# A two-block transformer on one core: attention heads of the second block beside its projections, and stage seams taken token tile by token tile

## The reference, cut to what matters

```python
# mixer A, token width 1024: 4 "diff" heads with two softmax maps each, 4 "moba" heads
h = x @ w_in                                  # 1024 x 3072
dq, dk, mq, mk = (apply_rope(...) of slices of h);  dv, mv = slices of h
s = where(kpos <= qpos, q @ k.T * scale, -inf);  p = softmax(s)
w = p[:, :, 0] - lam_full * p[:, :, 1]        # diff: the two maps joined
a = rms_norm_2(w @ dv, subln) * (1 - lambda_init)
b = softmax(causal(mq @ mk.T * scale)) @ mv   # moba: with 256 tokens one block, plain causal attention
x = layer_norm(ALPHA * x + concat(a, b) @ w_out)
x = layer_norm(ALPHA * x + square(relu(x @ w1)) @ w2)          # FFN, inner width 4096
# mixer B, gated linear attention (GLA): q, k (512 wide), v, r (1024), 16 gate columns
g = log_sigmoid(h16 @ w_gate_up + b_gate) / 16                  # decay of every key column
o = causal linear attention of q, k, v with the decays exp(cumsum(g))
x = layer_norm(ALPHA * x + (rms_norm_2(o) * silu(r)) @ w_out)
x = layer_norm(ALPHA * x + square(relu(x @ w1)) @ w2)           # second FFN; its result is the output
```

## Time and profile before

| | |
|---|---|
| median of three runs | 1716.16 us (1713.0 to 1716.29) |
| the profiled execution | 1713.44 us, of which the span from first to last instruction is 1711.6 us |
| mean granted clock of TensorE in it | 0.940 of full speed |
| PE busy | 1380.6 us (81% of the span) |
| DVE busy | 1131.3 us (66%) |
| ACT busy | 539.2 us (32%) |
| POOL busy | 454.7 us (27%) |
| weights and experts read from HBM | 431.00 MB, 252 GB/s over the span |

### The profile page before, as it was taken

One profiled execution on the slowest core, in us unless ns is written; L12 is line 12 of the kernel. 1 busy time (PEld: TensorE's weight loads), 2 busy tenths in 40 slices (PEclk: granted clock), 3 DMA queues, 4 the chain that ended last, 5 costly groups with the idle time before them and its releaser, 6 DMA issues.

```text
span 1711.6 us, 17345 instructions
## 1 busy us (share of the span) xinstructions
PE 1380.6 (81%) x6264; PEld 971.9 (57%) x6264; DVE 1131.3 (66%) x2051; ACT 539.2 (32%) x1023; POOL 454.7 (27%) x393
## 2 busy tenths in 40 slices
PE   6976788777777677777777788658999899789998
PEld 5875668523223232222222267547999687679996
DVE  6655665688887788886555556647756659577564
ACT  2453434222221213212111233323434246234341
POOL 1154305244443443544444200000211025001110
PEclk9988899999998999999999989878999999889999
DMA  9554526799999999999999823204555534245550
GB/s 367 190 184 148 196 74 227 293 421 409 421 421 412 421 408 382 400 422 420 422 421 421 344 75 123 98 25 142 182 196 197 189 110 147 75 151 179 188 197 25
DMA packets 116629, 433.17 MB, mean 253 GB/s; under 512 B 6832, under 2 KB 7088, under 8 KB 83520
## 3 DMA queue, kind: packets, MB, share of 16 engines
q0 software_dynamic: 36864, 268.45, 38.0%
q1 hardware_dynamic: 79392, 162.51, 26.8%
q10 hardware_dynamic: 288, 1.11, 0.2%
HBM read 431.00 MB, written 1.05 MB: 252 GB/s over the span
## 4 chain that ended last, share of the span: by engine, by line
PE 47%; DMA 23%; DVE 19%; ACT 6%; issue 2%; POOL 2%; SPq 0%; DVEq 0%; ACTq 0%; POOLq 0%
PE PS L45 45%; DMA EB<-in_experts,EI 22%; DVE EB L78 5%; DVE WL L75 3%; ACT BIG L24 2%; PE PS L84 1%; DVE X L63 1%; POOL W L75 1%; ACT WH L24 1%; DVE Y L75 1%; DMA W<-in_w_ada 1%; DVE GV L75 1%; DVE EB L63 1%; DVE XL L75 1%; DVE ST L69 1%
## 5 line engine op out<-in xcount | busy, mean ns | idle before, releaser
L45 PE MATMUL PS<-EB,BIG 128*128 128x512 f32 x1024 | 495.4, 628 | 169.9 <-ACT BIG L24 169.8
L45 PEld LDWEIGHTS PS<-EB,BIG 128*128 128x128 f32 x1024 | 190.3, 197 | 470.3 <-ACT BIG L24 287.3
L78 DVE CUSTOM_DVE_ANT_0 EB<-EB,Y 128x1024 f32<-128x1024 f32 x256 | 313.4, 1224 | 146.0 <-DMA EB<-in_experts,EI 145.0
L39 POOL DMA_INDIRECT EB<-in_experts,EI x256 | 288.3, 1126 | 397.0 <-PE PS L45 380.9
L75 DVE TENSOR_TENSOR WL<-W,WH 128x1024 fp32r<-128x1024 f32 x228 | 297.5, 1351 | 109.5 <-ACT WH L24 109.3
L45 PE MATMUL PS<-XH,WH 128*128 128x256 f32 x928 | 272.0, 293 | 12.8 <-DVE WL L75 10.0
L24 ACT ACTIVATE WH<-W 128x1024 fp32r<-128x1024 f32 x240 | 237.8, 1047 | 91.8 <-PE PS L45 84.9
L45 PE MATMUL PS<-XL,WH 128*128 128x256 f32 x928 | 265.0, 286 | 0.0
L45 PE MATMUL PS<-XH,WL 128*128 128x256 f32 x928 | 265.0, 286 | 0.0
L45 PEld LDWEIGHTS PS<-XH,WH 128*128 128x128 f32 x928 | 180.9, 195 | 17.9 <-DVE WL L75 11.1
L45 PEld LDWEIGHTS PS<-XL,WH 128*128 128x128 f32 x928 | 180.8, 195 | 2.7 <-issue 2.4
(11 more groups left out here) (170 smaller groups left out, 1512.1 us busy)
## 6 DMA issues: line engine op xcount, KB each, us to landing
W<-in_ffn_w SPq DMA_DIRECT2D x32, 2048.0 KB, 8.8
W<-in_w_ada SPq DMA_DIRECT2D x12, 2048.0 KB, 12.2
W<-in_w_in SPq DMA_DIRECT2D x6, 2048.0 KB, 12.9
W<-in_hy_w_in SPq DMA_DIRECT2D x6, 2048.0 KB, 13.5
W<-in_gla_w_in SPq DMA_DIRECT2D x6, 2048.0 KB, 7.9
W<-in_w_query SPq DMA_DIRECT2D x4, 2048.0 KB, 8.2
W<-in_w_out SPq DMA_DIRECT2D x2, 2048.0 KB, 8.3
EB<-in_experts,EI POOLq DMA_INDIRECT x256, 11.1
```

The costliest lines, as they stand in the source:

```text
L39: return lambda e: e.indirect_dma_start(*a, **k)
L45: return lambda e: e.matmul(*a, **k)
L78: return lambda e: e.tensor_tensor_reduce(*a, **k)
```

## The change

The second block's order of work is rewritten in four places; no product is dropped.

1. *Splits.* Eleven weight tiles (44 pieces) have their low half computed on POOL and no longer on DVE.
2. *Mixer A.* The rotation of a rope pair is recorded one group later, the copy · cos on POOL, the sum one group after that. The scores' mask is added in PSUM by a product of an identity with the mask (both fp32r, 384 columns). DVE only reduces the maximum from PSUM, and ACT takes the exponentials straight from PSUM. The two maps of a diff head are joined by products with diagonal matrices (ACT writes 1/sum and −lam/sum onto the identity, six f32 products per head), which also turn them, so three transposes and DVE's joining fall away. The diff heads are recorded between the projection groups 10 to 16; the moba heads behind the 16th and inside hy_out, whose k loop is cut in two: the diff half first, the moba half last.
3. *Seams.* The first tile behind three layer norms (FFN up tile of both FFNs, gla_in[0]) is computed in token form, t = 0 before the transposes of t = 1 and t = 1 behind them; its result is transposed back (eight transposes).
4. *GLA.* The first step of `levels` is recorded before the turning of the queries and gla_in[1]; values come before gates; the last gate tile's second half is cut in three parts around the last levels and the heads; the heads' norm begins on t = 0 while t = 1 is still open, and t = 1 is turned inside gla_out.

```diff
+        on_pool = [*hy_out, *(ffn_tiles[0][0][0, j] for j in range(2)), gla_in[0], gla_in[1], gla_in[5], *gla_out,
+                   *(ffn_tiles[1][0][0, j] for j in range(2))]
         for t in tiles[hyt[2].index:]:
-            later_split(t)
+            later_split(t, pool if t in on_pool else None)
...
+        act(lambda e: e.activation(mask_r, maskF, ACT.Copy), t_k1, q_done[3], ordered=False)
+        t_mr = act(lambda e: e.activation(ident_r, ident, ACT.Copy), t_k1, q_done[3], ordered=False)
+        blocks = [slice(i * 128, (i + 1) * 128) for i in range(3)]
+        cols = [slice(0, 128), slice(128, 384)]
...
+        def exponents(q, k, b, L, j, *tokens):
+
+            pe.wait(*tokens, t_mr, *bank_free[b])
+            pe.plain(lambda e: e.matmul(PS[b][:, 0:384], ident_r, mask_r, start=True, stop=False))
+            pe.plain(lambda e: e.matmul(PS[b][:, 0:128], q[:, 0:128], k[:, 0:128], start=False, stop=False))
+            tk = pe(lambda e: e.matmul(PS[b][:, 128:384], q[:, 128:256], k, start=False, stop=True), ordered=False)
+            for t in range(2):
+                tm = dve(lambda e: e.tensor_reduce(MXA[:, j + t:j + t + 1], PS[b][:, cols[t]], X_AXIS, ALU.max, negate=True), tk, ordered=False)
+            for t in range(2):
+                ta = act(lambda e: e.activation(L[:, cols[t]], PS[b][:, cols[t]], ACT.Exp, bias=MXA[:, j + t:j + t + 1],
+                                                accum_out=SMA[:, j + t:j + t + 1]), tm, ordered=False)
+            bank_free[b] = (ta,)
+            return ta
...
+        def diff_scores(h):
+            c = h - h % 2
+            for m in range(2):
+                i = 2 * h + m
+                heads["d", h] = exponents(QD[:, i, :], KD[:, h, :], 6 + m, buf(i), 2 * i, roped["dq", c], roped["dk", c])
+            j = 4 * h
+            dve(lambda e: e.reciprocal(SMA[:, j:j + 4], SMA[:, j:j + 4]), heads["d", h])
+            td = dve(lambda e: e.tensor_tensor(SMA[:, j + 2:j + 4], SMA[:, j + 2:j + 4], lam.broadcast_to([128, 2]), ALU.mult))
+            for n in range(4):
+                ta = act(lambda e: e.activation(D2[h % 2][:, blocks_of[n]], ident, ACT.Copy, scale=SMA[:, j + n:j + n + 1]), td, *d2_free[h % 2],
+                         ordered=False)
+            heads["d", h] = ta
...
+        def diff_turned(h):
+            b = bank()
+            for i in range(3):
+                t = min(i, 1)
+                tt = mm(PS[b][:, blocks[i]], [(buf(2 * h + m)[:, blocks[i]], D2[h % 2][:, blocks_of[2 * m + t]]) for m in range(2)],
+                        heads["d", h], *bank_free[b])
+            d2_free[h % 2] = (tt,)
+            pe.wait(*dp_free[h % 2])
+            heads["dt", h] = put_turned(h, b, buf(8 + h % 2), tt)
...
+        fresh = [0]
+        beside = {10: ((diff_scores, 0),), 11: ((diff_scores, 1),), 12: ((diff_turned, 0), (diff_scores, 2)),
+                  13: ((diff_turned, 1), (diff_values, 0), (diff_scores, 3)), 14: ((diff_turned, 2), (diff_values, 1)),
+                  15: ((diff_turned, 3), (diff_values, 2)), 16: ((diff_values, 3), (moba_scores, 0), (moba_scores, 1))}
+
+        def behind_group():
+
+            fresh[0] += 1
+            while adding:
+                adding.popleft()()
+            if fresh[0] % 2 and turning:
+                turning.popleft()()
+            for f, h in beside.get(fresh[0], ()):
+                f(h)
+
+        fm_tile(hyt[2], evac_rope("dq", r64, c64, s64, fin_split, 0.125), *t_xt, hook=behind_group)
+        fm_tile(hyt[3], evac_rope("dk", r64, c64, s64, fin_to(KD)), hook=behind_group)
+        fm_tile(hyt[4], evac_rope("mq", r128, c128, s128, fin_to(QM), 128.0 ** -0.5), hook=behind_group)
+        fm_tile(hyt[5], evac_rope("mk", r128, c128, s128, fin_to(KM)), hook=behind_group)
+        turning.popleft()()
...
+        t_moba = {}
+        diff_steps, diff_x = norm_half(0, write_diff, 4, 1e-5, subln)
+        tick(2)
+        moba_turned(0, bank())
+        moba_turned(1, bank())
+        adding.popleft()()
+        diff_steps[0]()
+        diff_steps[1]()
+        moba_scores(2)
+        moba_scores(3)
+        diff_steps[2]()
+        diff_steps[3]()
+        moba_values(0)
+        moba_values(1)
+        tick(2)
+        diff_steps[4]()
+        dve(lambda e: e.reciprocal(SMA[:, 16:24], SMA[:, 16:24]), heads["m", 3])
+        diff_steps[5]()
+        diff_steps[6]()
+        tick(2)
```

The order inside hy_out, and the token form behind a norm with its users:

```diff
+        def both_tiles(tile, before, evac=lambda t, b, tk: None):
+
+
+            done = []
+            for t in range(2):
+                if t:
+                    before.last()
+                b = bank()
+                tk = dense(PS[b][:, :], take(tile), tm_pairs(tile, t), before.xt[t], *bank_free[b])
+                if t:
+                    wdone(tile, tk)
+                done.append(evac(t, b, tk))
+                tick(2)
+            return done
...
+            def turn_tokens(t):
+                r, ta = squares[t]
+                ts = slice(t * 128, (t + 1) * 128)
+                b = bank()
+                for c in range(4):
+                    tk = tr(PS[b][:, c * 128:(c + 1) * 128], r[:, c * 128:(c + 1) * 128], ta, *bank_free[b])
+                hi, lo = (a[:, 0, 0:4, ts] for a in (AH, AL))
+                ps = PS[b][:, :].rearrange("p (c t) -> p c t", c=4)
+                th = act(lambda e: e.activation(hi, ps, ACT.Copy), tk, *at_free[0], ordered=False)
+                tl = dve(lambda e: e.tensor_tensor(lo, ps, hi.bitcast(F32), ALU.subtract), th, ordered=False)
+                bank_free[b] = (tl,)
+                y_free[t] = (tk,)
+                at_first.append(tl)
...
+        for t in range(2):
+            for j in range(2):
+                b = bank()
+                groups[j, t] = b
+                filling.add(b)
+                dense(PS[b][:, :], take(hy_out[j]), tm_pairs(hy_out[j], t), diff_x["x", t], *bank_free[b], ks=range(4), stop=False)
+                if (j, t) == (0, 0):
+                    moba_turned(2, 4)
+                    moba_turned(3, 5)
+                    tick(2)
+                if (j, t) == (1, 0):
+                    moba_values(2)
+                    moba_values(3)
+                    wh_free[ffn_tiles[0][0][0, 0].index] = (heads["mv"],)
+                    wh_held.clear()
+                    tick(2)
+                if (j, t) == (0, 1):
+                    write_moba(0)
+                    write_moba(1)
+                    tick(2)
+        for t in range(2):
+            for j in range(2):
+                b = groups[j, t]
+                filling.discard(b)
+                tk = dense(PS[b][:, :], hy_out[j], tm_pairs(hy_out[j], t), t_moba[t], ks=range(4, 8), start=False,
+                           mid=norm_mix.mid if (j, t) == (1, 1) else None)
+                if t == 1:
+                    wdone(hy_out[j], tk)
+                norm_mix.give(j, b, t, tk, turn=False)
+                if (j, t) != (1, 1):
+                    tick(2)
```

GLA:

```diff
-        fm_tile(gla_in[0], evac_flat(0, 128.0 ** -0.5), *t_xt)
         t_bg2 = gate_sums()
-        fm_tile(gla_in[1], evac_flat(1024, 1.0))
+        lv = levels()
+        next(lv)
+        for t in range(2):
+            e_free[0] = e_free[1] = (turn_query(t),)
+            tick(2)
+        fm_tile(gla_in[1], evac_flat(1024, 1.0), *t_xt)
         t_qk = act.last
-        lv = levels()
         next(lv)
...
         for j in range(2):
-            tm_tile(gla_in[4 + j], with_levels(evac_silu(j)), n=2)
-        for j in range(2):
             tm_tile(gla_in[2 + j], with_levels(evac_tok(lambda t: VG[:, t, j * 512:(j + 1) * 512])), n=2)
+        t_v = (act.last, dve.last)
+        tm_tile(gla_in[4], with_levels(evac_silu(0)), n=2)
+        last_gate = take(gla_in[5])
+        b = bank()
+        tk = dense(PS[b][:, :], last_gate, tm_pairs(last_gate, 0), *bank_free[b])
+        bank_free[b] = with_levels(evac_silu(1))(b, 0, tk)
+        t_sg = [pool.last]
+        tick(2)
+        b_gate = bank()
+        filling.add(b_gate)
+
+        def gate_part(ks):
+            return dense(PS[b_gate][:, :], last_gate, tm_pairs(last_gate, 1), *bank_free[b_gate], ks=ks, start=ks[0] == 0, stop=ks[-1] == 7)
+
+
+        gate_part(range(0, 3))
+        next(lv)
+        gate_part(range(3, 5))
         for _ in lv:
...
+        tk_gate = gate_part(range(5, 8))
+        filling.discard(b_gate)
+        wdone(last_gate, tk_gate)
...
+        ready = head_norm(0, head_squares(0))
+        t_square = head_squares(1)
+        bank_free[b_gate] = evac_silu(1)(b_gate, 1, tk_gate)
+        after.pop()()
+        t_sg.append(pool.last)
+        x_heads = [turn_tile(Y[:, 0, :], 0, ready)]
+        ready = head_norm(1, t_square)
```

More of the change, by code:

```diff
@@ L322, in build @@
         ffn_tiles = [plan_ffn(0)]
-        gla_in = {j: wplan_on(A["gla_w_in_2"], 0, j) for j in (0, 1, 4, 5, 2, 3)}
+        gla_in = {j: wplan_on(A["gla_w_in_2"], 0, j) for j in range(6)}
         gla_out = [wplan_on(A["gla_w_out_2"], 0, j) for j in range(2)]
@@ L1563, in build @@
```

(47 more changed lines are left out.)

182 lines of the change are left out of this document (115 added, 67 removed).

## The result

The changed kernel takes 1703.36 us in the median of four runs (1702.3 to 1704.51), the kernel before in the same session 1716.22 (1713.0 to 1717.26): ratio 0.9928, 95% interval 0.9911 to 0.9946. So it is faster, by 12.9 us and not by the 36 that were forecast. The profiled execution took 1702.68 us, its span is 1700.9 us, 10.7 shorter than the one before.

A forecast was written before the change was run, and what follows sets the result against it. Bound by PE inside the stages and a DVE–ACT–DVE chain around heads and seams. +7.8 − 36.7 − 3 + 5.0 − 8.3 + 1.0 = −34.2 on 1713.4 gives 1679.2, 1680 for a median; range 1665 to 1692.

The forecast's parts named there:

- POOL's price: Cost on the path of the 44 low-half pieces moved to POOL: about 4 us taken, at worst 43.
- B: Heads to the end of hy_out and its norm's first half, 88.1 us before: 51.4 forecast, −36.7.
- E: GLA's levels, heads and norm, 84.4 us before: 76.1 forecast, −8.3; second token tile's turning inside gla_out, +1.0.
- A: Mixer A's projections to the end of the 16th group, 62.1 us before: 69.9 forecast, +7.8.
- score set: Term of the projections: one map's score products plus mask product, 0.90 us each, eight sets 7.2.
- C: Two seams into an FFN, 22.2 us each before: 19.9 each, plus 0.8 for POOL, together −3.
- D: Start of GLA, 39.7 us before: +5.0, PE waiting for key copies queued on ACT behind the first decays' exponential.
- Rival 2: Blocks in ACT's queue at the seams and GLA's start don't hurt: 1665 us, chance 0.20.
- Rival 1: Diff heads not hidden between the projections, ACT late: the 16.1 us of waits come back, 1696; chance 0.20.
- Rival 3: POOL's pieces decide, delaying decays, rope products and DVE's two-input passes: 43 us, 1722; chance 0.05.
- restart: Term for PE's slower matmuls after an idle: about 2.2 us lost each time, read from 11 matmuls.

The follow-up runs named there:

- e2: The kernel before, with only the same eleven tiles' low halves moved to POOL: 1732.8 us, ratio 1.0096 to the kernel before.
- e1: The changed kernel with all 44 low halves back on DVE, order otherwise the same: 1694.02 us, ratio 0.9874 to the kernel before.
- e5: The changed kernel with POOL kept only for the twelve pieces split before the first norm, the other 32 back on DVE: 1685.05 us.
- e6: The changed kernel with the edits of e3, e4 and e5 together: 1661.03 us, ratio 0.9689 to the kernel before.
- e7: The changed kernel with the diff heads' steps in the same order but all behind the 16th projection group: 1708.82 us.
- e11: e7 with the mask added by DVE while copying the scores to SBUF, in place of the product on PE: 1714.89 us.
- e4: The changed kernel with the second token half's turning recorded ahead of the first half's evacuation and two weight pieces at three seams: 1688.3 us.
- e3: The changed kernel with the first step of GLA's levels (first decays) recorded behind the keys' tile, as before the change: 1695.59 us.

## Why the prediction was right in direction and wrong in size

**The step that failed** is "POOL's price", with its "I take about 4 of it (2 in B, 0.8 a seam): most pieces are split a tile ahead, beside PE's dense work". The pieces are beside PE's dense work, but so are the passes of the norm's first token tile, on DVE, and PE waits for these. I priced a piece by what it adds to a DVE pass of its own length (0.97), while it adds its whole length to a pass of one column. On the kernel before this part alone costs 17 us (e2), 20.1 by the profiles, in three lots of about 7 at the three norms. In the changed kernel, taking all pieces off POOL gives 9.3 (e1), taking off the 32 late ones 18.3 (e5), and e5's 1685 lies in the forecast's own range. Behind mixer A e5 gives DVE back all of its load and still gains 16.9, so there it is not DVE's load that costs, but POOL's pieces at the norms and the late ones below.
The rule of the Trainium skill ("SBUF — State Buffer", section "Who interferes with whom") is that a DVE instruction with two SBUF inputs contends with a GpSimd instruction that reads SBUF, and one with at most one SBUF input does not. The traces agree: 2.19 for 0.16 in the first case, 0.65 for 0.65 in the second. The sum by it was to be 7 us more, with one meeting per norm; the trace has four in a row (2.0, 4.3 and 2.0 us over the time alone), and the lower clock behind PE's wait comes on top (e2).

**The rest of the late pieces.** At the second FFN PE also waits for POOL directly, 3.41 and 2.30 us. POOL, then PE:

```profile
1517.95 5.62 POOL L75 TENSOR_TENSOR WL<-W,WH 128x1024 fp32r<-128x1024 f32 x2 [7.89 <-ACT WH L24]
```

```profile
1520.35 0.39 PE L45 MATMUL PS<-XH,WH 128*128 128x256 f32 x1 [3.41 <-POOL WL L75]
1523.63 0.58 PE L45 MATMUL PS<-XH,WH 128*128 128x256 f32 x1 [2.30 <-POOL WL L75]
```

POOL had stood for 7.89 us at ACT's copies, recorded behind the square of the second half. On DVE (e1, e6) 2.4 are left of the 5.7. In all B fell short by 3.1, the first FFN by 6.7, gla_out by 7.5 and the second seam by 6.8; E fell short by 3.8, and comes 3.3 nearer in e1: PE's longest wait there, 4.59 us for a level's operands, is 2.00 without POOL's pieces. The new order of GLA's tiles was tested by no run of its own.

**A and B were right, for a partly wrong reason.** The end of the 16th group and hy_out's start came out within 3 us, B's length within 3.1. A score set with its mask took 0.73 (two from 1054.31 to 1055.78), not 0.90, with 0.17 and 0.37 from each mask's start to that of its scores. But the waits of 16.1 us did not go only because the heads stand between the projections: e7 takes that away, and loses 6.5 in the stage. The mask product, with scores that stay in PSUM, is worth 4.8 there (e11, over all twelve maps). The rest goes to the joining by diagonals or to several maps being in flight; which of the two was not tried.

**C was right in its own terms** (first seam: 19.4 and 1.2 of turning back, against 22.2 and a forecast of 20.7 with POOL's share) and so was the mechanism, weight pieces on ACT ahead of XH (e4). **D was right**: forecast a wait of 8 to 9 us before the diagonal products, measured 7.48, released by the key copies; e3 leaves 0.69 of it. Rival 2 said that these blocks would not hurt; they did. Rival 1 did not come: PE works for 65.56 of the projections' 67.56 us, and even with the heads behind them (e7) 6.5 and not 16.1 would have come back. Rival 3 named DVE's delayed two-input passes, and had the wrong size: POOL's late pieces ate 18 of the 34 us, not all of them.

Three readings of the prediction were off without consequence. The heads joined between the groups are four, as in its sum, not three as in the sentence before it. D's terms up to the scans add up to 31.7, not 32.1. Between the two rows stand ten products, so a restart there is about 1.9 us, not 2.2.

**With the three losses taken out** the way from the table's start to the end is 50.5 us shorter than before (e6), more than the 34.2 forecast for the change as it stands.

## What to carry to other kernels

Before work is moved from DVE to an idle POOL, look at which short DVE passes on the critical path have two sources in SBUF and will run at the same time: here the price was a whole piece of 2.3 us per pass that met one, not a share of the piece, and PE's lower clock after the wait on top. Move it where DVE reads PSUM or does nothing urgent (here: ahead of the first norm, worth 13.6 us), and leave it where a norm's chain runs. In an in-order queue, a wait recorded early is paid by all that stands behind it: a copy that releases PE belongs ahead of optional work such as weight pieces and of an exponential that waits for another engine.

## What had not been expected of the hardware

The same instructions of PE take different times in two runs, by when the clock comes back after an idle. Between hy_out's start and the first norm's transposes e3 has the changed kernel's queue, and hy_out starts behind the same wait of 4.40 us. Products of 512 columns are 0.43 us apart at the lower of the clock's two levels (1.2 GHz) and 0.23 at the upper one (2.4 GHz). In the changed kernel the lower level ends 1.9 us behind hy_out's first product, in e3 4.8 us behind it; and a wait of 2.14 us in the middle of hy_out is followed by it in e3 only. The mean granted clock is 0.93 in the changed kernel and 0.84 in e3, the stretches are 3.2 us apart. Busy times by stretch, the changed kernel and e3:

```profile
1107.40:1139.00 31.60, 24.81 (x116) 19.89 (x115) 13.69 (x19) 8.66 (x12) 14.11 (x6) 0.93 0.26 87
```

```profile
1107.40:1142.20 34.80, 27.78 (x116) 22.12 (x115) 13.92 (x19) 8.62 (x12) 14.11 (x6) 0.84 0.23 80
```

PE's busy time differs by 2.97 us for the same 116 instructions, DVE's, ACT's and POOL's by at most 0.23. An idle that is removed can so give back more than its length (in e2 5.27 us of wait brought 2.1 of slower work), and by how much is not the same each time: 3 us between two single profiles of one stage can be the clock's alone.
